# A scan whose output is made turned, with its raw blocks' stores on two queues and its first loads moved ahead

## The reference

```python
def trunk_layer(x, mod, s0, grid, lp, router_w, router_b):
    h = rms_norm(x, lp['norm1_g']) * (1 + sc1) + sh1
    mix, s_final = parallel_mixer(h, s0, grid, lp)     # conv, RWKV scan and chunked MLP, gated and summed
    x = x + ga1 * mix
    h = rms_norm(x, lp['norm2_g']) * (1 + sc2) + sh2
    x = x + ga2 * routed_moe(h, ...)                   # 16 experts, 2 of them for each token
# the scan, forward and backward over the tokens, 8 heads of 64:
def step(S, inp):
    r_t, w_t, k_t, v_t, kk_t, kka_t = inp
    sa = jnp.einsum('bdhvk,bdhk->bdhv', S, kk_t)
    S = S * w_t[..., None, :] - sa[..., :, None] * kka_t[..., None, :] + v_t[..., :, None] * k_t[..., None, :]
    return S, jnp.einsum('bdhvk,bdhk->bdhv', S, r_t)
# afterwards, for each token and head: y = y_forward + y_backward, less its mean, over its deviation, scaled,
# plus rk * v (the "bonus", rk the sum over a head of r * k_dir * r_k), times a gate
```

## Time and profile before

| | us |
|---|---|
| median of 3 timed runs (lowest, highest) | 4027.17 (4001.73, 4028.21) |
| the profiled execution's own time | 3987.78 |
| its span, first to last instruction | 3986.0 |
| PE busy in the span | 3632.5 (91%) |
| DVE, POOL, ACT busy | 1378.7, 1079.8, 783.3 |
| mean granted TensorE clock | 0.948 |

### The profile page before, as it was taken

The page is one execution under the profiler, slowest core; times in us unless marked ns, Lnnn a source line. Parts: engine busy times, 40 slices in busy tenths (PEclk is TensorE's granted clock), DMA queues, the critical chain, the costliest instruction groups (busy, mean ns, idle before and its releaser), DMA issues. The chain is left out here.

```text
span 3986.0 us, 64120 instructions
## 1 busy us (share of the span) xinstructions
PE 3632.5 (91%) x24967; PEld 2877.3 (72%) x24968; DVE 1378.7 (35%) x2811; ACT 783.3 (20%) x1467; POOL 1079.8 (27%) x1573
## 2 busy tenths in 40 slices
PE   8999999995799999999799999999999949999960
PEld 4777666663699889999788989989989934444420
DVE  2444444442345454454122222222222242222237
ACT  1222222222233333232111111111111101111113
POOL 0333333333555555555011011011011000000013
PEclk9999999997899999999899999999999969999985
DMA  8323222223323333332711011111011144765235
GB/s 290 106 100 105 97 95 91 91 96 136 88 74 97 102 101 101 95 91 52 244 69 64 35 41 64 35 41 64 35 41 64 41 166 164 258 230 185 89 111 206
DMA packets 297255, 424.33 MB, mean 106 GB/s; under 512 B 122446, under 2 KB 206156, under 8 KB 297036
## 3 DMA queue, kind: packets, MB, share of 16 engines
q1 hardware_dynamic: 268812, 309.84, 23.8%
q10 hardware_dynamic: 16272, 67.64, 4.5%
q0 software_dynamic: 11952, 43.52, 3.3%
HBM read 287.99 MB, written 132.94 MB: 106 GB/s over the span
## 5 line engine op out<-in xcount | busy, mean ns | idle before, releaser
L1757 PE MATMUL c_ps<-c_hT,big 128*128 128x128 f32 x6528 | 751.3, 276 | 27.3 <-DMA big<-in_w_in 27.3
L1757 PEld LDWEIGHTS c_ps<-c_hT,big 128*128 128x128 f32 x6528 | 742.6, 193 | 35.3 <-issue 30.1
L661 PE MATMUL a_ps<-a_win,a_hT 128*128 128x512 f32 (+1 forms) x1088 | 416.1, 540 | 3.8 <-DVE a_mix L572 3.8
L2180 PE MATMUL e_ps<-big,e_xT 128*128 x784 | 347.6, 597 | 2.3 <-DVE e_xT L2142 2.3
L661 PEld LDWEIGHTS a_ps<-a_win,a_hT 128*128 128x128 f32 x1088 | 204.0, 190 | 199.8 <-issue 187.0
L655 PE MATMUL a_ps<-a_hT,a_win 128*128 128x128 f32 x2992 | 343.9, 277 | 2.3 <-ACT a_hT L343 2.3
L655 PEld LDWEIGHTS a_ps<-a_hT,a_win 128*128 128x128 f32 x2992 | 340.6, 193 | 6.2 <-issue 2.9
L1110 POOL TENSOR_TENSOR b_tmp<-b_tt,b_ta 128x126 f32<-128x126 f32 (+22 forms) x527 | 203.7, 386 | 332.4 <-DMA b_ta<-s_a 269.5
L2180 PEld LDWEIGHTS e_ps<-big,e_xT 128*128 128x128 f32 x784 | 149.4, 191 | 191.8 <-issue 191.8
L1757 PE MATMUL c_ps<-c_wo,c_mT 128*128 128x512 f32 x544 | 236.3, 592 | 0.0
L1722 DVE TENSOR_TENSOR c_gs<-c_gs,c_ps 128x384 f32<-128x384 f32 x136 | 75.3, 554 | 445.1 <-PE c_ps L1757 434.9
(11 more groups left out here) (328 smaller groups left out, 5338.3 us busy)
## 6 DMA issues: line engine op xcount, KB each, us to landing
big<-in_exp_w SPq DMA_DIRECT2D x48, 1024.0 KB, 10.3
s_D<-a_shared SPq DMA_DIRECT2D x34, 768.0 KB, 5.9
s_yr<-e_yo ACTq DMA_DIRECT2D x49, 512.0 KB, 3.1
b_f<-s_D ACTq DMA_DIRECT2D x32, 768.0 KB, 7.9
a_aw<-in_ada_w SPq DMA_DIRECT2D x32, 512.0 KB, 6.6
b_f<-s_A ACTq DMA_DIRECT2D x32, 512.0 KB, 5.7
s_A<-a_shared SPq DMA_DIRECT2D x17, 768.0 KB, 3.4
big<-in_w_in SPq DMA_DIRECT2D x12, 1024.0 KB, 12.3
```

Of the source, the lines that this page charges most:

```text
L661: ins = nc.tensor.matmul(ps[:, bank, 0:width], hT[b][:, k, :], win[:, k, c:c + width], start=k == 0, stop=k == KD - 1)
L1757: return nc.tensor.matmul(out, lhsT, rhs, start=start, stop=stop)
L2180: return nc.tensor.matmul(out, lhsT, rhs, start=start, stop=stop)
```

## The change

- The output product in the scan exchanges its operands: `Shd` is stationary and `RT` moves, and of `V` and `Us` 64 columns are stationary while `ArkT` and `ArbT` move with 128 columns; the two heads of a j write to partitions 0 to 63 and 64 to 127. `Y0` and `Y1` then hold features on partitions.
- In the merge PE turns the sum back (`turn_y`: four transposes into `WB[1]`), for tile t+1 behind `project(2)` of tile t, and for tile 0 behind its `gates(0)`; `scan_center` reads that bank. In tile 0 all of `gates(1)` to `gates(3)` stand before the transposes of the normalised y.
- SP's order in a step becomes: the inverse's store (`inverse_out(q)`), the four forward raw blocks of q+1, the inverse's return (`inverse_in(q)`), the load of `TA` (`diagonal_in(q + 1)`). The four backward blocks go out from ACT (`backward_out`), between its raw copies and `identity`.
- `a_win` and the scan's `F`, constants and some of its tiles share one piece of memory that lives through both stages (`front`). SP issues the loads of the first fronts and of all constants in the last tile of the token stage, after the last use of the weights and ahead of that tile's stores; their semaphores live as long.
- In the last tile of the token stage the row products, the bonus and their sum are DVE's.
- `invert(0)` is DVE's, ahead of its step 0; `invert(1)` to `invert(16)` stay POOL's.

```diff
@@ stage_tokens, sync, step
+                    if last:
+                        sp.wait_ge(s["ident_in"], 16)
+                        for name in GROUPS:
+                            after(sp, s[name], t)
+                        for name in ("stA", "stD0", "stD1"):
+                            sp.wait_ge(s[name], 16 * LAT)
+                        for d in range(2):
+                            load_front(sp, io, scr, K, (0, LAT - 1)[d], d)
+                        sp.dma_start(K["const"][:, :, :], io["consts"]).then_inc(K["const_in"], 16)
                     sp.wait_ge(s["ident_in"], 16)
                     after(sp, s["conv_ok"], t)
@@ stage_tokens, vector, step (and the same five operations left out of gpsimd's where last)
+                    if last:
+                        after(dve, s["kd1"], t)
+                        nc.vector.tensor_tensor(rsum[:, :], oD[0][:, 0, :], oD[1][:, 0, :], ALU.add).then_inc(s["s1"], 1)
...
                     nc.vector.reduce_sum(rk8[:, :], rsum[:, :].rearrange("p (h n) -> p h n", h=H), axis=X_AXIS)\
                         .then_inc(s["rk_ok"], 1)
+                    if last:
...
+                        nc.vector.tensor_tensor(oO[:, 0, :], oO[:, 0, :], lxb[:, :], ALU.add).then_inc(s["bonus_ok"], 1)
@@ stage_scan
+        def diagonal_out(e, d, tile):
+            for i in range(4):
+                own = slice(SB * i, SB * i + SB)
+                at = 32 * d + 8 * i
+                e.dma_start(scr["a32"][at:at + 8].rearrange("s (r c) -> r s c", r=SB), tile[own, :, own]).then_inc(a_st, 16)
@@ sync
+                def forward_out(t, b):
+                    sp.wait_ge(const_in, 16)
+                    after(sp, ar_ok[0][0], t)
+                    after(sp, ar_ok[0][1], t)
+                    diagonal_out(sp, 0, Ar[0][b])
...
+                    inverse_out(q)
+                    if left > 0:
+                        forward_out(q + 1, 1 - b)
                     inverse_in(q)
                     if left > 0:
-                        diagonal_out(q + 1, 1 - b)
+                        diagonal_in(q + 1)
@@ scalar
+                def backward_out(t):
+                    after(act, at_ok, t, 2)
+                    if not (isinstance(t, int) and t == 0):
+                        after(act, ta_in, t - 1, 32)
+                    diagonal_out(act, 1, AT)
...
                 raw(0, 0)
+                backward_out(0)
...
                         raw(q + 1, 1 - b)
+                        backward_out(q + 1)
                         identity(q + 1)
@@ gpsimd, vector
-                invert(0)
...
+                invert(dve, v_, 0)
@@ tensor, step
-                            mm(bank(d, 1)[:, j * P:(j + 1) * P], RT[d][:, j, :], Shd[d][:, j, :], stop=False)
-                            for h in (2 * j, 2 * j + 1):
-                                own = slice(h * N, (h + 1) * N)
-                                mm(bank(d, 1)[:, own], ArkT[d][:, slot(h), :], V[d][b][:, own], start=False, stop=False)
-                                ins = mm(bank(d, 1)[:, own], ArbT[d][:, slot(h), :], Us[d][:, own], start=False, stop=h % 2 == 1)
+                            at = bank(d, 1)[:, j * P:(j + 1) * P]
+                            mm(at, Shd[d][:, j, :], RT[d][:, j, :], stop=False)
+                            for mix, val in ((ArkT, V[d][b]), (ArbT, Us[d])):
+                                for u in range(2):
+                                    h = 2 * j + u
+                                    ins = mm(at[64 * u:64 * u + 64], val[:, h * N:(h + 1) * N], mix[d][:, slot(h), :],
+                                             start=False, stop=mix is ArbT)
@@ stage_merge, tensor
+                def turn_y(t):
+                    after(pe, s["ysum"], t)
+                    freed(pe, s["yT_ok"], t)
+                    for k in range(4):
+                        ins = nc.tensor.transpose(ps[:, WB[1], k * P:(k + 1) * P], ya[:, k * P:(k + 1) * P], ident)
+                    ins.then_inc(s["yt_ps"], 1)
...
                     for j in range(KD):
                         project(j)
+                        if j == 2 and left > 0:
+                            turn_y(t + 1)
                         if j + 4 < KD:
                             gates(j + 4)
```

More of the change, by code:

```diff
@@ L137, in stage_tokens @@
         ident = K["ident"][:, :]
-        win = sb("a_win", [P, KD, CGATE])
+        win = K["front"][:, :].rearrange("p (k n) -> p k n", k=KD)
         lw = sb("a_lora_w", [P, W])
@@ L780, in stage_scan, with from_front, by_four, from_front2 @@
         ps = ctx.enter_context(nc.psum_tensor("b_ps", [P, 8, 512], F32))
-        const = sb("b_const", [P, NCONST, P])
+        const = K["const"]
         ident = K["ident"][:, :]
-        F = each("f", [P, 5, W])
+        F = K["F"]
         FR, FKK, FKD, FKA, FSG = range(5)
-        V = each2("v", [P, W])
-        EI, EN, EX = each("ei", [P, W]), each("en", [P, W]), each("ex", [P, W])
-        PM, fac = each2("pm", [P, 4, 2]), each("fac", [P, 4])
[L788 to L791, removed]
+        home = iter(K["rest"])
+        def from_front(n):
+            return [next(home) for i in range(n)]
+        def by_four(ap):
+            return ap.rearrange("p (j n) -> p j n", j=4)
+        def from_front2():
+            return [from_front(2) for d in range(2)]
+        V = from_front2()
+        EI, EN, EX = from_front(2), from_front(2), from_front(2)
+        PM, fac = each2("pm", [P, 4, 2]), each("fac", [P, 4])
+        Qt, Rt = from_front(2), from_front(2)
+        Bt, Kt = from_front2(), from_front2()
+        QT, RT, KT = ([by_four(ap) for ap in from_front(n)] for n in (4, 2, 2))
+        QT = [QT[0:2], QT[2:4]]
+        BT = each2("bT", [P, 4, P])
         Ar, AT = each2("ar", [P, H, P]), sb("b_at", [P, H, P])
@@ L981, in front @@
                         after(act, pm_ps[d], t - 1)
-                        load_front(act, tiles[d], d)
+                        load_front(act, io, scr, K, tiles[d], d)
                 def turned(t, b):
@@ L1805, in step @@
                     gates(0)
+                    if first(t):
+                        turn_y(0)
                     gates(1)
+                    if first(t):
+                        gates(2)
+                        gates(3)
                     after(pe, s["yf_ok"], t)
                     freed(pe, s["mix_ok"], t, 2)
+                    after(pe, s["yc_ok"], t)
                     for k in range(4):
@@ L1811, in step @@
                     ins.then_inc(s["yT_ps"], 1)
-                    gates(2)
                     if not first(t):
+                        gates(2)
                         turn_h2(t - 1)
-                    gates(3)
-                    if not first(t):
+                        gates(3)
                         logits(t - 1)
@@ L1830, in step @@
                         freed(pe, s["mix_ok"], t, 2)
+                        if i == 1 and left > 0:
+                            after(pe, s["yc_ok"], t + 1)
                         for k in range(KD):
@@ L2376, in program @@
              "gs": ctx.enter_context(nc.sbuf_tensor("gs", [P, 2, 2, KD], F32))}
-        stage_tokens(nc, io, scr, K)
-        stage_scan(nc, io, scr, K)
         across = Sems(nc, ctx)
+        K["const_in"], K["f_in"] = across("const_in"), [across(f"f_in{d}") for d in range(2)]
+        with ExitStack() as both:
+            front = both.enter_context(nc.sbuf_tensor("front", [P, KD * CGATE], F32))
+            K["front"] = front
+            tile = 5 * W
+            K["F"] = [front[:, d * tile:(d + 1) * tile].rearrange("p (a n) -> p a n", a=5) for d in range(2)]
+            rest = 2 * tile + NCONST * P
+            K["const"] = front[:, 2 * tile:rest].rearrange("p (a n) -> p a n", a=NCONST)
+            K["rest"] = [front[:, at:at + W] for at in range(rest, KD * CGATE, W)]
+            stage_tokens(nc, io, scr, K)
+            stage_scan(nc, io, scr, K)
         K["rc_in"], K["early_in"] = across("rc_in"), across("early_in")
```

138 lines of the change are left out of this document (69 added, 69 removed).

## The result

The changed kernel takes 4030.3 us, median of 20 runs, against 3992.7 for the kernel before, also of 20; ratio 1.009, 95% interval 1.0071 to 1.0109. It is slower by 38 us, inside 1% and inside the range, but I had forecast 14 us faster. The profiled execution of the changed kernel took 4021.25 us, span 4019.2.

The account below looks back on a forecast made before the run. TensorE was taken to bound the scan (busy 801 of 843 us) and merge (1198 of 1203), loads and small work the entry. Terms -15.0 + 7.5 + 15.1 - 16.7 - 2.9 - 2.0 = -14.0 us: 4013 us from 4027.2, range 3976 to 4050.

Parts of the forecast that it names:

- Raw blocks' stores: Scan steps 1 to 16: later TZ issue cancels against avoiding the fronts' loads, and waits for TZ go; -2 us.
- rival 2: Scan: TZ behind the raw stores lands as much later as issued, PE waits in 16 steps; +70, 4083 us; chance 0.08.
- Clock: Scan: granted clock 0.96 on average, 34 us lost, carried over; none hit would give 3979 us, chance 0.08.
- twice: Clock rival in the scan: twice as many steps hit by the low clock, 4047 us; chance 0.09.
- Output made turned: Scan's output product: a j takes 1.00 us instead of 1.11, 0.88 us a step over 17 steps, -15.0 us.
- Rivals 1 and 5: Scan output: 1, switches cost nothing, -60 us, chance 0.07; 5, halves don't overlap, +26 us, chance 0.03.
- The merge: Merge: four more transposes per tile on PE, +7.5 us, and the turn's wait in tile 0, +15.1 us.
- the wait in tile 0: Merge's first tile: PE waits 13.4 us for tile 1's sum, plus 1.7 us for the lower clock; +15.1 us.
- Rival 4: Merge's first tile: Y lands earlier, so no wait for the turn; 3998 us; chance 0.10.
- The entry: Token stage's end to scan: closing stores begin 4.5 us earlier, scan work starts 12.2 us earlier; together -16.7 us.
- Step 0: Scan's first step: first product to the inverse's second half takes 73.0 us instead of 75.9, VectorE's inversion 20; -2.9 us.

Follow-up runs that it names:

- the entry alone: Changed kernel with the raw blocks' stores put back in steps 1 to 16 and the output and merge as before: 3975.6 us, 0.9936.
- the pair of moves in the kernel before: Kernel before with only the raw stores split: forward four on SP before TZ, backward four on ACT before the fronts' loads: 4054.0 us, 1.013.
- all four edits: Changed kernel with TZ before forward stores, early Y loads in the merge's first tile, AT's transposes behind Aqk's masks, fronts before the wait for AT: 3946.0 us, 0.9875.

## Why the prediction was wrong, step by step

**Raw blocks' stores: wrong, and nearly the whole of the miss.** I put them at -2 us; they cost 47 in the changed kernel and 59 by themselves. The step that failed is "I take that the two cancel": TZ issued 4.4 us later, but ahead of the fronts' loads instead of into them. It is not ahead of them. Its eight loads take 3.78 us to issue (the earlier trace rows had 4.15), and the fronts start 2.27 us into that; before they started 1.44 us into it. My own numbers gave that away: TZ from 1462.2 on for 4.15 us ends at 1466.4, and the fronts, some 3 us and four stores (2.1 us) behind the last raw copy at 1460.11, start at 1465.2. Measured from the end of the raw copies (1460.11 in step 8 of before, 1466.45 in the same step after), TZ's first load goes out 5.7 us later (1457.78 and 1469.81), the fronts' first 6.5 us later (1459.22 and 1472.08), and TZ's last piece lands 6.3 us later (1470.65 and 1483.32). The fronts' first load in the kernel before:

```profile
1459.22 0.35 ACTq L866 DMA_DIRECT2D b_f<-s_A  x1
```

The whole bunch has moved as one, and TensorE had no slack there. The fronts I had set down as "wanted only later": they are, but I did not ask what else is in flight when they now go out. The load of the raw blocks lies under them too; its median to landing, with TZ's beside it (DMA issues, KB each, us to landing), shows where a median helps and where not:

```profile
b_ta<-s_a SPq DMA_DIRECT2D x30, 256.0 KB, 10.8
b_tz<-s_t SPq DMA_DIRECT2D x120, 32.0 KB, 2.1
```

With all stores back the raw blocks' load takes 3.9 us. TZ's 2.1 us looks harmless, since only the last two of eight pieces are late.

My rival 2, slower through TZ, had the right place and sign and got 0.08. Its reason, the later issue alone, was not the right one: with the fronts later still, the same late TZ costs nothing.

**Clock: a second part of the loss in these two profiles, its cause open.** I carried the 34 us of the earlier trace rows over unchanged, with "twice" as a rival. It became 126 us at half clock instead of 75, worth up to 26 us (a half clock beneath a wait costs nothing). In the changed kernel its place moves to the new wait in seven steps: two windows of step 8, on the masks' wait and at the wait for TZ.

```profile
1463.00:1473.00 10.00, 8.19 (x136) 7.91 (x134) 6.91 (x12) 3.56 (x7) 3.49 (x3) 1.00 0.28 43
1483.00:1493.00 10.00, 8.84 (x60) 8.73 (x61) 3.53 (x6) 4.60 (x9) 5.58 (x18) 0.72 0.45 135
```

Waits 37.8 - 2.0, clock 26 and output -15 make 47 us, against 40.8 measured from first to last y. That the late TZ brought the longer half clock is not shown: with TZ first, and no wait for it, 116 us are at half clock, with the entry alone 130. Executions of one kernel differ as well: the mean granted clock of the kernel before goes from 0.935 to 0.953 (0.944 on average over its executions on record; 0.9415 with the change).

**Output made turned: right.** 1.00 us a j predicted, 1.00 measured. Two steps have neither a wait for TZ nor half clock in either trace, the third from the end and the last: from y to y they go from 50.15 to 49.26 us and from 43.01 to 42.00, -0.89 and -1.01 against -0.88. Rivals 1 and 5 are out. One j's two changes between the full array and its halves cost 0.33 us (1.00 against 0.67). That agrees with the drain at a change of tiling mode that the Trainium skill's page TensorEngine Tiling (Array Packing) names under "Key Properties".

**The merge: right.** Predicted +22.6 us, measured +21.8 from its first to its last product; the wait in tile 0 is 14.45 us against 13.4, and putting Y's loads earlier gives it back. The 7.3 us around the merge were no part of the sum. Rival 4 is out.

**The entry: right.** -16.7 predicted and -16.8 measured up to the first product. Step 0 reaches the second half of the inverse 73.3 us after the first product (953.36 to 1026.70, 73.0 predicted), and its inversion on VectorE takes 21.7 us (20 predicted). The run with the entry alone gains 19 us in all by the medians.

Without the stores the sum is -12.0 us; the run with the stores put back gained 12.3 (interval 6 to 22). The agreement is partly luck: the half clock of that run is 24 us longer than before, and other terms made up for it.

What stays open: why one step falls to half clock behind a wait and the next does not. Of the 15 steps with a masks' wait of 1.7 to 1.9 us, half clock follows that wait in six before, in ten with TZ first, in one with the fronts ahead of the wait for AT, and in none with the pair of moves in the kernel before.

## What to carry to other kernels

When a wait is put in front of transfers, ask not only when they are wanted but what else will be in flight when they now go out: here a 2.5 MB load, first read 19.6 us after it went out (1472.08 to 1491.64 in step 8), came to lie on the last 64 KB of one that TensorE was waiting for. A gather of many small pieces is as late as its last piece; a median to landing hides it. And of two moves that each cost little, the pair has to be costed as a pair.

## What the runs showed that I had not expected

TensorE's half clock mostly came under or behind a wait, and where it came changed with the waits: 13 to 15 us into a step with the masks' wait of 1.7 us, 22 to 27 us with the wait for TZ of 4 to 6, 32 to 39 us with one of 1.34. Taking the masks' wait away therefore did not make the kernel faster where another wait took its place (0.91 over the scan in that profile). But the masks' wait does not have to go: with the fronts ahead of the wait for AT it stands at 26.6 us as before, and the scan's clock is 0.98 (37 us at half clock, in the fastest of twelve executions), as good as with all four edits:

```profile
1061.74:1893.05 831.31, 771.37 (x8163) 700.48 (x8161) 405.15 (x685) 278.71 (x531) 444.74 (x990) 0.98 0.32 90
```

Four VectorE operations in a row of the first inversion (two products and two sums, 993.79 to 998.83) took 1.23 to 1.24 us each, where others of their size took 0.27 to 0.29, while POOL ran four products beside them (993.50 to 998.68).
